# A streaming-encoder block on one core: experts chosen tile by tile inside the mixer, the router fed by transposed h, slot tables built without GpSimd, gates gathered from memory per expert

## The chip, the core and the metric

The kernel runs on one core of one Trainium2 chip. The metric is the device time of one execution in microseconds, as the median of several runs. The core has five engines that work side by side and meet at semaphores: TensorE (PE; PEld is its weight load), VectorE (DVE), ScalarE (ACT), GpSimd (POOL) and SyncE (SP, which here only issues DMAs). PSUM has 8 banks, into which PE writes and from which DVE and ACT read.

## The reference, cut to what matters

One layer over 2048 tokens of width 1024, batch 1, in float32:

```python
u = rms_norm(x, norm1_w)
z = u @ w_in + b_in                      # GLA q,k,v,g, low rank; sliding-window q,k,v
x = x + concat(gla(z), swa(z)) @ w_out   # "the mixer"
hf = rms_norm(x, norm2_w)
gp = softmax(hf @ w_group + b_group)     # 4 groups
g_w, g_idx = top_k(gp, 1)
el = (hf @ w_router + b_router)[group g_idx]   # 8 experts in the chosen group
e_val, e_idx = top_k(el, 2)
gate = softmax(e_val) * g_w
x = x + sum over the 2 chosen of gate * ((silu(hf @ w_gate[e]) * (hf @ w_up[e])) @ w_down[e])
y = rms_norm(x, final_norm_w)
```

There are 32 experts with an inner width of 512; the 2048 tokens make 4096 assignments, 128 per expert on average.

## The kernel before, in words

The program has four stages, each written once per engine.

**The mixer** works on 16 tiles of 128 tokens as a software pipeline: `pipeline` runs turns i = 0, 1, then a loop over pairs for 2 to 15, then 16 and 17. The table `JOBS` gives the PE jobs with their lag (turn i works on tile i - lag), the semaphore that says when a job's PSUM bank has been read, and, by the place in the table, the bank: job k writes bank k mod 8. Before it writes, a job waits (`bank_free`) until the job 8 places earlier (the table taken as a ring that goes on into the turn before) has been read. So a job's place in the table decides whom it waits for. In one turn PE does the projections `qk`, `v`, `g`, `kv`, `qb`, the transposes and small matmuls of both attentions, then `wo0` and `wo1` (output projection), the scores `s0` to `s3`, `bb` and `bl`. DVE adds the output projection to x and gets h (L711), ACT squares h, POOL makes the reciprocal root (L749, L751), DVE scales h to v2 (L738), and SP stores h and v2. In the next turn PE transposes v2 (`u2Ta`, `u2Tb`, L282), DVE copies the transposes to u2T (L638), and PE multiplies them with the router's weights (L373). DVE adds the bias; `logits` keeps all 16 tiles.

**Routing** follows when all 16 tiles are through: DVE picks the group and the two experts for all tiles in one long chain (L922 to L961), PE counts and ranks (L882 to L884), DVE turns ranks into slots and makes two one-hot tables, `place` and `column` (L993), POOL multiplies `column` by token numbers (L1036) and by gates (L1042), and PE sums both over the tokens (L889, L896). The results are, per slot: which token to gather (`idx`), where to add the result (`put`) and its gate (`weight`), and `meta`, the width class of each expert.

**Experts**: a loop over 32 experts. For each, POOL adds back the rows of the expert before (`put_back`, indirect DMA with add, L1087), gathers the rows of the next (L1109 128 rows of 4 KB, L1111 128 quarter rows of 1 KB), and SP loads three weight matrices of 2 MB into one buffer as soon as each has been used. PE does 32 gate matmuls (L1168) and 32 up matmuls (L1179), transposes the next expert's rows (L1136), and does the down projection (L1204). A matmul of float32 shows as two rows, so a group of 32 shows as x64. An expert with up to 128 tokens takes width 128, others 144 or 160; the rest goes to overflow chunks.

**The final norm** reads h back, scales it and stores the output.

Of the kernel before, what the change touches and what calls it, by code (L numbers as in the profile page):

```python
# [17 lines left out]
F32 = mybir.dt.float32  # L18
# [57 lines left out]
class Semaphores:  # L76
# [16 lines left out]
    ("u2Ta", 2, {"u2T_ready": (2, 1)}), ("u2Tb", 2, {"u2T_ready": (2, 2)}),  # L93
# [15 lines left out]
]  # L109
INDEX = {name: k for k, (name, _, _) in enumerate(JOBS)}  # L110


def mixer(nc, sem, bank, A, C, scratch, ctx):
# [23 lines left out]
    xn = sb("xn", [P, D])  # L137
# [10 lines left out]
    la_t = sb("la_t", [P, QKA])  # L148
    g_t = sb("g_t", [P, VA])
    ls = sb("ls_sb", [P, QKA])  # L150
# [26 lines left out]
    def loads(sp):  # L177

        sp.dma_start(x[:, :], A["x"][0:P, :]).then_inc(sem("x_loaded"), 16)
        for lo, hi in ((0, C_V), (C_V, C_G), (C_G, C_LR), (C_LR, IN_W)):  # L180
# [5 lines left out]
            if lo == C_V:  # L186
                sp.wait_ge(sem("xn_ready"), 1)
                sp.dma_start(x[:, :], A["x"][P:2 * P, :]).then_inc(sem("x_loaded"), 16)
# [42 lines left out]
    def sp_iter(sp, i, par):  # L231

        if not isinstance(i, int) or 1 <= i < NT - 1:
            wait_apart(sp, rider, (sem("xn_ready"), i + 1))
            nxt = i + 1 if isinstance(i, int) else (i + 1) & (NT - 1)
            sp.dma_start(x[:, :], tile_rows(A["x"], nxt)).then_inc(sem("x_loaded"), 16)
        if not isinstance(i, int) or i < NT:
            if isinstance(i, int) and i == 1:
                clear_spare(sp)
            wait_apart(sp, rider, (sem("h_stored"), 16 * (i - 1)),  # L240
# [28 lines left out]
    def pe_iter(pe, i, par):  # L269
# [27 lines left out]
        def transpose_x(t):  # L297

            wait(pe, sem("xn_ready"), t + 1)
            transposes("xTa", lambda c: xn[:, c * P:(c + 1) * P], 4)  # L300
            if not (isinstance(t, int) and t == 0):
                on("xTb")
            transposes("xTb", lambda c: xn[:, (4 + c) * P:(5 + c) * P], 4)
# [33 lines left out]
        if on("u2Ta"):  # L337
            wait(pe, sem("v2_ready"), i - 1)
            transposes("u2Ta", lambda c: v2[:, c * P:(c + 1) * P], 4)
        if on("u2Tb"):  # L340
            transposes("u2Tb", lambda c: v2[:, (4 + c) * P:(5 + c) * P], 4)

# [129 lines left out]
        if on("bl"):  # L472
# [3 lines left out]
            m.then_inc(sem("bl_done"), 1)  # L476

# [3 lines left out]
    def act_iter(act, i, par):  # L481
# [51 lines left out]
        if new:  # L533
# [5 lines left out]
            wait(act, sem("ls_ready"), i)  # L539
# [37 lines left out]

    def dve_iter(v_, i, par):
# [5 lines left out]
        def normalise_x(t):  # L584
# [3 lines left out]
            dve.tensor_scalar(xn[:, :], x[:, :], ss[:, 1:2], None, ALU.mult).then_inc(sem("xn_ready"), 1)  # L588
# [101 lines left out]
        if new:  # L690
# [10 lines left out]
            wait(v_, sem("bl_done"), i)  # L701
# [4 lines left out]
        if old:  # L706
            wait(v_, sem("xr_loaded"), 16 * i)
            for n in range(2):
                wait(v_, sem("wo_done"), 2 * (i - 1) + n + 1)
                hs = h[:, 1 - par, n * 512:(n + 1) * 512]  # L710
                dve.tensor_tensor(hs, BK[f"wo{n}"][:, :], hs, ALU.add).then_inc(sem("h_ready"), 1)  # L711
        if new:
# [12 lines left out]
            if isinstance(i, int) and i == 0:  # L725
                dve.memset(sc[:, :, 0:CHUNK], NEG).then_inc(sem("filled"), 1)
                v_.wait_ge(sem("filled"), 6)
# [6 lines left out]
        if old:  # L734
            wait(v_, sem("rstd2_ready"), i)
            wait(v_, sem("v2_stored"), 16 * (i - 1))
            wait(v_, sem("u2Tb_done"), i - 1)
            dve.tensor_scalar(v2[:, :], h[:, 1 - par, :], ss[:, 9:10], None, ALU.mult).then_inc(sem("v2_ready"), 1)  # L738


    def pool_iter(po, i, par):
# [19 lines left out]
        if old:  # L761
# [3 lines left out]
                 (sem("v2_ready"), i - 1))  # L765
# [25 lines left out]
def host_constants():  # L791
# [17 lines left out]
        "c_rank": (j < i).astype(np.float32) - 1.0,  # L809
        "c_tie": np.tile(np.arange(EPG, 0, -1, dtype=np.float32), (P, 1)),  # L810
        "c_cols": np.tile(np.arange(NE, dtype=np.float32) * CAP, (P, 1)),
        "c_ovj": np.arange(NOV, dtype=np.float32)[None, :],
        "c_tok": (1 + np.arange(NT)[None, :] * P + np.arange(P)[:, None]).astype(np.float32),
        "c_rep": np.concatenate([np.tile(np.eye(P, TAIL, dtype=np.float32), (1, P // TAIL)),
                                 np.arange(P, dtype=np.float32)[:, None] // TAIL,
                                 (SEQ + 1 + np.arange(2) * P + np.arange(P)[:, None])], 1).astype(np.float32),
# [4 lines left out]
def routing(nc, sem, bank, A, K, scratch, ctx):  # L821
# [5 lines left out]
    rank_c = sb("rank_c", [P, P])  # L827
    ones = sb("ones", [P, P])
    cols = sb("cols", [P, NE])
    ovj = sb("ovj", [1, NOV])  # L830
    tok = sb("tok", [P, NT])
    iota = sb("iota", [P, P])
    rep = sb("rep", [P, P + 3])
    NCOL = NSLOT // P
    column_t = sb("column_t", [P, 2 * NT, NCOL])
    idx_f = sb("idx_f", [P, NE])
    empty = sb("empty", [P, NCOL])
    put_f = sb("put_f", [P, NCOL])
    spread = sb("spread", [P, 2, NE])
    place = sb("place", [P, 2 * NT, P])  # L840
    column = sb("column", [P, 2 * NT, NCOL])
    lof, hif = sb("slot_lo_f", [P, 2 * NT]), sb("slot_hi_f", [P, 2 * NT])
    gmax, wsum, gw = sb("gmax", [P, NT]), sb("wsum", [P, NT]), sb("gw", [P, NT])
    eg, ohg, pg = sb("eg", [P, NT, NG]), sb("ohg", [P, NT, NG]), sb("pg", [P, NT, NG])
    big = sb("big", [P, NT, NE])
    el, te = sb("el", [P, NT, EPG]), sb("te", [P, NT, EPG])
    oh = sb("oh", [P, 2, NT, EPG])
    mx = sb("mx", [P, 2, NT])
    OH = sb("OH", [P, 2, NT, NE])
    OHs, OHcum = sb("OHs", [P, NE, NT]), sb("OHcum", [P, NE, NT])  # L850
    later = sb("later", [P, NE, NT])
    tot, cnt, nov, cumov, base = (sb(n, [P, NE]) for n in ("tot", "cnt", "nov", "cumov", "base"))
    novi = sb("novi", [P, NE], I32)
    one_row = sb("one_row", [P, NE])
    slot = sb("slot", [P, 2, NT])
    lo, hi = (sb(n, [P, 2, NT], I32) for n in ("slot_lo", "slot_hi"))
    ovc, meta_f = sb("ovc", [1, NOV, NE]), sb("meta_f", [1, NE + NOV + 1])
    logits, gates, dest, idx, meta = K["logits"], K["gates"], K["dest"], K["idx"], K["meta"]
    tie, put, weight = K["tie"], K["put"], K["weight"]

    def sp_loads(sp):

        wait(sp, sem("logits_ready"), NT)
        sp.wait_ge(sem("v2_stored"), 16 * NT)
# [4 lines left out]

    def act_part(act):  # L870
# [666 lines left out]
```

## Time and profile before

| | us |
|---|---|
| median of 3 runs | 1891.57 |
| lowest and highest run | 1891.21 and 1893.16 |
| the profiled execution, its own time | 1888.9 |
| its span, first to last instruction | 1887.0 |
| PE busy in the span | 1768.8 |
| DVE, ACT, POOL busy | 526.2, 495.3, 297.6 |
| mean granted clock of PE | 0.97 |

All durations below come from the profiled execution. Its time is 1.9 us more than its span and 2.7 us less than the median. A busy PE may still work at half its clock, and matmuls overlap each other, so the share of busy time says where PE never waits, not how well it is used. The times of a timeline count from the start of the span.

### The profile page before, as it was taken

How to read it: one execution, taken by the hardware profiler on the slowest of the kernel's cores; microseconds unless marked ns; L12 is line 12 of the kernel's file. 1: busy time of each engine (PE TensorE's matmuls, PEld its weight loads, DVE VectorE, ACT ScalarE, POOL GpSimd, SP SyncE). 2: the span in 40 equal slices, each digit the busy share in tenths (PEclk: the TensorE clock that was granted, in tenths of full speed). 3: DMA queues.
4: the chain of work that ended last, by engine and by line, in shares of the span. 5: the costliest groups of instructions: out<-in, count | busy, mean ns of one | idle time of the engine just before them, and what ended most of it. 6: DMA issues, size and time to landing. Idle time of an engine off the chain costs nothing. (4 is left out here: it accounts for less than half of the span.)

```text
span 1887.0 us, 28465 instructions
## 1 busy us (share of the span) xinstructions
PE 1768.8 (94%) x10628; PEld 1265.9 (67%) x10629; DVE 526.2 (28%) x1089; ACT 495.3 (26%) x1221; POOL 297.6 (16%) x353
## 2 busy tenths in 40 slices
PE   7999999999999999999973899999999999999980
PEld 4556665666656666566642788888888888888860
DVE  1333233332433323342237211111111111111114
ACT  0434343442333433333320111111111111111114
POOL 0000011010110101001012312222222222222223
PEclk9999999999999999999996899999999999999995
DMA  9411011110111001110023489999999899999969
GB/s 325 91 45 46 7 38 44 44 43 2 44 44 44 22 22 44 44 44 11 33 86 108 158 284 330 315 302 313 317 314 328 268 340 314 311 314 316 310 199 361
DMA packets 127760, 312.86 MB, mean 166 GB/s; under 512 B 10179, under 2 KB 18388, under 8 KB 127732
## 3 DMA queue, kind: packets, MB, share of 16 engines
q1 hardware_dynamic: 111460, 269.79, 40.4%
q0 software_dynamic: 15552, 42.61, 9.0%
q8 instruction: 19, 0.31, 0.1%
q10 hardware_dynamic: 720, 0.08, 0.0%
q14 instruction: 9, 0.07, 0.0%
HBM read 265.27 MB, written 47.19 MB: 166 GB/s over the span
## 5 line engine op out<-in xcount | busy, mean ns | idle before, releaser
L287 PE MATMUL bank<-w_in_sb,uT 128*128 128x512 f32 (+1 forms) x1024 | 378.6, 523 | 0.9 <-DVE uT L595 0.9
L287 PEld LDWEIGHTS bank<-w_in_sb,uT 128*128 128x128 f32 x1024 | 176.3, 192 | 168.5 <-issue 168.5
L1168 PEld LDWEIGHTS bank<-xT,wts 128*128 128x128 f32 x2048 | 250.4, 192 | 21.5 <-issue 17.1
L1168 PE MATMUL bank<-xT,wts 128*128 128x128 f32 (+2 forms) x2048 | 254.4, 284 | 3.0 <-issue 1.9
L1179 PE MATMUL bank<-xT,wts 128*128 128x128 f32 (+2 forms) x2048 | 247.9, 282 | 0.0
L1179 PEld LDWEIGHTS bank<-xT,wts 128*128 128x128 f32 x2048 | 245.0, 191 | 0.0
L1204 PE MATMUL bank<-wts,hT 128*128 128x512 f32 x512 | 231.7, 595 | 0.0
L318 PE MATMUL bank<-w_out_sb,mixT 128*128 128x512 f32 x512 | 222.7, 593 | 1.5 <-ACT mixT L517 0.8
L318 PEld LDWEIGHTS bank<-w_out_sb,mixT 128*128 128x128 f32 x512 | 95.9, 190 | 116.5 <-issue 114.3
L1257 DVE TENSOR_TENSOR hT<-bank,sg 128x160 f32<-128x160 f32 x128 | 41.5, 324 | 442.1 <-PE bank L1179 442.1
L1204 PEld LDWEIGHTS bank<-wts,hT 128*128 128x128 f32 x512 | 92.2, 190 | 97.6 <-issue 97.6
L293 PEld LDWEIGHTS bank<-uT,w_in_sb 128*128 128x128 f32 x1280 | 147.9, 192 | 11.9 <-issue 11.6
L293 PE MATMUL bank<-uT,w_in_sb 128*128 128x128 f32 x1280 | 155.7, 277 | 0.0
L749 POOL TENSOR_SCALAR ss<-ss 128x1 f32<-128x1 f32 (+1 forms) x49 | 9.4, 193 | 844.6 <-issue 430.2
L1087 POOL DMA_INDIRECT h_dram<-y,putc x64 | 102.1, 1595 | 35.9 <-POOL putc L1094 26.2
L1223 ACT ACTIVATE y<-bank,gatec 128x256 f32<-128x256 f32 x32 | 15.2, 474 | 344.1 <-PE bank L1204 198.0
L1214 ACT ACT_TABLE_LOAD x32 | 41.1, 1283 | 203.1 <-PE bank L1168 203.1
L1094 POOL COPY putc<-put 128x2 int32 (+1 forms) x32 | 5.9, 184 | 532.9 <-DVE y L1265 532.9
L711 DVE TENSOR_TENSOR h_sb<-bank,h_sb 128x512 f32<-128x512 f32 x32 | 22.1, 692 | 188.3 <-PE bank L318 188.3
L1214 ACT ACTIVATE sg<-bank 128x160 f32<-128x160 f32 x128 | 38.9, 304 | 117.7 <-PE bank L1168 117.3
L574 ACT ACTIVATE sc<-sc,sm 128x192 f32<-128x192 f32 x128 | 56.3, 441 | 32.9 <-DVE sm L733 32.9
L560 ACT ACTIVATE junk<-h_sb 128x1024 bf16<-128x1024 f32 x16 | 16.9, 1057 | 147.8 <-DVE h_sb L711 147.8
(230 smaller groups left out, 1736.5 us busy)
## 6 DMA issues: line engine op xcount, KB each, us to landing
wts<-w_gate_in SPq DMA_DIRECT2D x32, 2048.0 KB, 10.8
wts<-w_up_in SPq DMA_DIRECT2D x32, 2048.0 KB, 9.3
wts<-w_down_in SPq DMA_DIRECT2D x32, 2048.0 KB, 9.0
x_sb<-x_in SPq DMA_DIRECT2D x17, 512.0 KB, 3.7
w_in_sb<-w_in_in SPq DMA_DIRECT2D x4, 2048.0 KB, 12.6
h_sb<-x_in SPq DMA_DIRECT2D x16, 512.0 KB, 4.5
h_dram<-h_sb SPq DMA_DIRECT2D x16, 512.0 KB, 2.7
v_dram<-v_sb SPq DMA_DIRECT2D x16, 512.0 KB, 2.9
```

The source lines that it names most:

```text
L287: m = pe.matmul(bk[name][:, col:col + hi - lo], uT[:, k, :], w_in[:, k, lo:hi], start=k == 0, stop=k == KD - 1)
L293: m = pe.matmul(bk[name][0:hi - lo, col:col + P], w_in[:, k, lo:hi], uT[:, k, :], start=k == 0, stop=k == KD - 1)
L318: m = pe.matmul(bk[f"wo{n}"][:, :], mixT[:, k, :], w_out[:, k, n * 512:(n + 1) * 512], start=k == HA, stop=k == HA - 1)
L560: act.activation(junk[:, :], h[:, 1 - par, :], ACT.Square, accum_out=ss[:, 8:9]).then_inc(sem("ss2_ready"), 1)
L574: act.activation(sc[:, hh, :], sc[:, hh, :], ACT.Exp, bias=nm[:, hh:hh + 1], accum_out=sums[:, hh:hh + 1])
L711: dve.tensor_tensor(hs, BK[f"wo{n}"][:, :], hs, ALU.add).then_inc(sem("h_ready"), 1)
L1087: po.indirect_dma_start(out=table, out_offset=bass.IndirectOffsetOnAxis(ap=putc[:, col:col + 1], axis=0), in_=src, in_offset=None, compute ...
L1168: m = pe.matmul(G[m_ % 2][:, 0:w], wg[:, k, m_ * P:(m_ + 1) * P], xT[:, k, 0:w], start=k == 0, stop=k == KD - 1)
L1179: m = pe.matmul(U[m_ % 2][:, 0:w], wu[:, k, m_ * P:(m_ + 1) * P], xT[:, k, 0:w], start=k == 0, stop=k == KD - 1)
L1204: m = pe.matmul(YB[half][:, :], hT[:, k, 0:P], wd[:, k, half * 512:(half + 1) * 512], start=k == 0, stop=k == KF - 1)
L1214: act.activation(sg[:, m_, 0:n_], G[m_ % 2][:, 0:n_], ACT.Silu).then_inc(sem(pre + "sg_ready"), 1)
L1257: nc.vector.tensor_tensor(hT[:, m_, 0:n_], U[m_ % 2][:, 0:n_], sg[:, m_, 0:n_], ALU.mult)\
```

## The change

It has five parts.

1. PE transposes h itself, not v2. The jobs `u2Ta` and `u2Tb` get lag 1 and move from place 2 and 3 of `JOBS` to its end, after `bl`. The router's output is now multiplied by the reciprocal root when DVE takes it from PSUM, together with the bias.
2. DVE chooses the experts of tile i-2 in turn i, with `choose` in two halves, ahead of the two residual additions. In the last turn both halves run at once, and only then v2 of the last tile is made.
3. x is normalised in place, la_t and ls share one buffer, so the next load of x waits for its transposes; the routing constants are loaded before the last two turns.
4. Routing needs no POOL: token numbers are put into `column` by one instruction per tile and choice (`tensor_scalar` with two operands), only one sum over tokens is left, and the gates are stored to memory by token, 2 for each.
5. In the experts, the gates of a chunk are fetched by two indirect DMAs (`load_gates`, 128 numbers of 4 bytes each) after the put-back of the chunk before.

```diff
 JOBS = [
     ("qk", 0, {"qk_ready": (1, 1)}), ("qdki", 1, {"qdkiT_ready": (1, 1)}),
-    ("u2Ta", 2, {"u2T_ready": (2, 1)}), ("u2Tb", 2, {"u2T_ready": (2, 2)}),
...
     ("bb", 0, {"decays_ready": (1, 1)}), ("bl", 0, {"dec_ready": (1, 1)}),
+    ("u2Ta", 1, {"u2T_ready": (2, 1)}), ("u2Tb", 1, {"u2T_ready": (2, 2)}),
 ]
...
+        for n, name in enumerate(("u2Ta", "u2Tb")):
+            if on(name):
+                wait(pe, sem("h_ready"), 2 * (i - 1) + n + 1)
+                transposes(name, lambda c: h[:, 1 - par, (4 * n + c) * P:(4 * n + c + 1) * P], 4)
...
+        if half == 0:
+            link(dve.tensor_reduce(mt[:, 0:1], L[:, 0:NG], AX.X, ALU.max))
...
+            link(dve.tensor_reduce(tm[:, :], te[:, :], AX.X, ALU.max))
+            return
+        link(dve.tensor_scalar(oh[:, 0, :], te[:, :], tm[:, :], None, ALU.is_equal))
...
+        dve.tensor_tensor(at(OHcum, t + 1), at(OHcum, t), at(OHs, t), ALU.add).then_inc(sem("choose_steps"), 1)
...
-            dve.tensor_tensor(dst, BK["router"][:, 0:NR], b_r[:, :], ALU.add).then_inc(sem("logits_ready"), 1)
+            wait(v_, sem("rstd2_ready"), i - 1)
+            dve.scalar_tensor_tensor(logits[:, :], BK["router"][:, 0:NR], ss[:, 9:10], b_r[:, :], ALU.mult, ALU.add)\
+                .then_inc(sem("logits_ready"), 1)
...
             for n in range(2):
+                if old2:
+                    if n == 0:
+                        wait(v_, sem("logits_ready"), i - 1)
+                    choose(v_, i - 2, n)
                 wait(v_, sem("wo_done"), 2 * (i - 1) + n + 1)
...
         for g in range(0, 2 * NT, PART):
-            for onehot, n, number in ((place, P, lof), (column, NCOL, hif)):
...
+            dve.tensor_tensor(place[:, g:g + PART, :], iota[:, None, :].to_broadcast([P, PART, P]),
+                              lof[:, g:g + PART].unsqueeze(2).to_broadcast([P, PART, P]), ALU.is_equal)
+            for n in range(g, g + PART):
+                m = dve.tensor_scalar(column[:, n, :], iota[:, 0:NCOL], hif[:, n:n + 1], tok[:, n:n + 1], ALU.is_equal, ALU.mult)
+            m.then_inc(sem("columns_ready"), 1)
...
+    def sp_gates(sp):
+        sp.wait_ge(sem("gates_ready"), 1)
+        sp.dma_start(scratch["gate"].rearrange("(t p n) o -> p t (n o)", p=P, n=2), gates[:, :, :]).then_inc(sem("gates_stored"), 16)
...
+    def load_gates(po, pre, at):
+
+        for part in range(2):
+            po.indirect_dma_start(out=gatec[:, part:part + 1], in_=scratch["gate"], out_offset=None,
+                                  in_offset=bass.IndirectOffsetOnAxis(ap=slotc[:, at + part:at + part + 1], axis=0))\
+                .then_inc(sem(pre + "gate_loaded"), 16)
...
+        put_back(po, "m_", y[:, 0, :], 0)
+        put_back(po, "m_", yt, 1, quarters=True)
+        load_gates(po, "m_", 2)
```

How PE's program stands in the loop over tiles, from the transposes of qd and ki to the `v` projection, before (L282 are `u2Ta` and `u2Tb`, L348 the GLA scores `att`, L359 the state update `dS`, L287 the `v` projection):

```order
L282 MATMUL bank<-ident,v_sb 128x128 [waits v2_ready,s_taken]
L282 MATMUL bank<-ident,v_sb 128x128 x3
L60 REGISTER_ALU
L282 MATMUL bank<-ident,v_sb 128x128 [waits s_taken]
L282 MATMUL bank<-ident,v_sb 128x128 x3
L60 REGISTER_ALU
L60 REGISTER_ALU [waits s_taken]
L348 MATMUL bank<-qdkiT 128x128 [waits qdkiT_ready,s_taken]
L348 MATMUL bank<-qdkiT 128x128 x3
L359 MATMUL bank<-v_sb,ke 64x128 [waits dec_ready,ke_ready,decays_ready,first_consts]
L359 MATMUL bank<-v_sb,ke 64x128 x7
L287 MATMUL bank<-w_in_sb,uT 128x512 [waits qdkiT_ready]
```

The same place now (line numbers of the changed kernel: L332 and L334 for qd and ki, L341 `att`, L352 `dS`, L286 the `v` projection):

```order
L332 MATMUL bank<-ident,qd 128x128 [waits qdki_ready,s_taken]
L332 MATMUL bank<-ident,qd 128x128
L334 MATMUL bank<-ident,ki 128x128 x2
L60 REGISTER_ALU
L60 REGISTER_ALU [waits s_taken]
L341 MATMUL bank<-qdkiT 128x128 [waits qdkiT_ready,s_taken]
L341 MATMUL bank<-qdkiT 128x128 x3
L352 MATMUL bank<-v_sb,ke 64x128 [waits dec_ready,ke_ready,decays_ready,first_consts]
L352 MATMUL bank<-v_sb,ke 64x128 x7
L60 ISA
L286 MATMUL bank<-w_in_sb,uT 128x512 [waits u2T_ready]
L286 MATMUL bank<-w_in_sb,uT 128x512 x7
```

The eight transposes are gone from between ki and `att` (they stand behind `bl`, ahead of the `qk` projection), and the `v` projection, which waited for the copy of qdkiT, now waits for u2T: it uses the bank of `u2Tb`. DVE's program has the two copies to u2T where they were, after the products with the softmax's sums and the addition to qk.

POOL's program in the loop over experts, before (copy of the gather's numbers, two gathers, copy of the put-back's numbers, two put-backs):

```order
L1122 COPY idxc<-idx 128x2
L66 REGISTER_ALU
L1109 DMA xg<-v_dram,idxc 128x1024 [waits m_index_ready,meta_ready]
L1111 DMA xg<-v_dram,idxc 128x256
L66 REGISTER_ALU
L1070 REGISTER_ALU [waits meta_ready,m_y_put]
L1070 REGISTER_ALU [waits m_yA_taken]
L1094 ISA [waits m_yD_taken]
L1094 COPY putc<-put 128x2
L1087 DMA h_dram<-y,putc 2304x1024 [waits m_put_index_ready,meta_ready]
L1087 DMA h_dram<-y,putc 9216x256
```

And now:

```order
L1118 COPY idxc<-idx 128x2
L66 REGISTER_ALU
L1105 DMA xg<-v_dram,idxc 128x1024 [waits m_index_ready,idx_ready]
L1107 DMA xg<-v_dram,idxc 128x256
L66 REGISTER_ALU
L1046 REGISTER_ALU [waits idx_ready,m_y_put]
L1046 REGISTER_ALU [waits m_yA_taken]
L1069 ISA [waits m_yD_taken]
L1069 COPY slotc<-tables 128x4
L1063 DMA h_dram<-y,slotc 2304x1024 [waits m_rows_ready,idx_ready]
L1063 DMA h_dram<-y,slotc 9216x256
L1075 DMA gatec<-gate_dram,slotc 128x1 x2
```

Two gathers of single numbers stand behind the put-backs, and so ahead of the gathers of the next turn.

## Rows read from the trace of the kernel before

**Rows 1.** Windows: stretch, length, busy us by engine (PE, PEld, DVE, ACT, POOL), clock, DMA share, GB/s.
```profile
200.00:300.00 100.00, 100.00 (x544) 64.13 (x543) 33.32 (x67) 37.51 (x92) 9.75 (x14) 1.00 0.07 27
...
980.00:1020.00 40.00, 14.57 (x43) 8.67 (x41) 22.23 (x58) 1.62 (x4) 0.74 (x2) 0.66 0.42 150
```

**Rows 2.** Timeline of one tile: start, us, engine, line, out<-in, idle before it.
```profile
898.92 0.38 PE L335 MATMUL bank<-ident,ki 128*128 128x128 f32 x2
...
899.14 1.04 PE L282 MATMUL bank<-ident,v_sb 128*128 128x128 f32 x8
...
899.34 0.60 ACT L495 ACTIVATE qdkiT<-bank 128x512 f32<-128x512 f32 x1
...
900.11 0.72 PE L348 MATMUL bank<-qdkiT 64*128 64x128 f32 x8
...
901.35 7.13 PE L287 MATMUL bank<-w_in_sb,uT 128*128 128x512 f32 x16
...
902.35 1.27 DVE L638 TENSOR_TENSOR u2T<-bank,norm_sb 128x512 f32<-128x512 f32 x2
```

**Rows 3.** Timeline: first tile's attention, and the second expert's start.
```profile
65.45 1.23 PE L348 MATMUL bank<-qdkiT 64*128 64x128 f32 x8 [2.94 <-ACT qdkiT L495]
...
67.67 8.78 PE L287 MATMUL bank<-w_in_sb,uT 128*128 128x512 f32 x16
...
1080.03 9.03 PE L1168 MATMUL bank<-xT,wts 128*128 128x128 f32 x64 [1.92 <-issue]
```

**Rows 4.** Timeline: DVE's residual additions in the loop and in the last tile.
```profile
882.24 0.69 DVE L711 TENSOR_TENSOR h_sb<-bank,h_sb 128x512 f32<-128x512 f32 x1 [5.58 <-PE bank L318]
...
985.22 0.69 DVE L711 TENSOR_TENSOR h_sb<-bank,h_sb 128x512 f32<-128x512 f32 x1 [2.67 <-PE bank L318]
```

**Rows 5.** Timeline from the last router matmuls to the first expert.
```profile
991.62 3.60 PE L373 MATMUL bank<-w_r_sb,u2T 128*128 128x36 f32 x16 [0.87 <-DVE u2T L638]
...
1008.97 2.08 PE L882 MATMUL bank<-OHs,rank_c 128*128 128x512 f32 x2 [13.76 <-DVE tot L961]
...
1013.28 0.18 DVE L966 TENSOR_SCALAR novi<-cnt 128x32 int32<-128x32 f32 x1
...
1014.85 0.69 DVE L976 TENSOR_SCALAR big<-bank 128x512 f32<-128x512 f32 x1
...
1021.27 1.22 DVE L993 TENSOR_TENSOR place<-iota,slot_lo_f 128x1024 f32<-128x1024 f32 x1
...
1023.43 1.22 DVE L993 TENSOR_TENSOR place<-iota,slot_lo_f 128x1024 f32<-128x1024 f32 x1
...
1052.16 1.04 PE L1136 MATMUL bank<-ident,xg 128*128 128x128 f32 x8
```

**Rows 6.** Timeline of one 128-wide expert: gathers, and transposes of what they bring.
```profile
1183.30 1.03 POOL L1109 DMA_INDIRECT xg<-v_dram,idxc  x1 [0.85 <-POOL idxc L1122]
...
1184.63 0.99 POOL L1111 DMA_INDIRECT xg<-v_dram,idxc  x1 [0.30 <-issue]
...
1191.18 1.04 PE L1136 MATMUL bank<-ident,xg 128*128 128x128 f32 x8
```

**Rows 7.** Windows: that expert, and one of width 144.
```profile
1176.60:1199.10 22.50, 22.50 (x155) 18.45 (x154) 3.82 (x9) 3.64 (x8) 5.58 (x6) 1.00 1.02 337
...
1226.50:1252.30 25.80, 25.80 (x187) 20.79 (x186) 3.82 (x9) 3.75 (x8) 5.59 (x6) 1.00 0.88 295
```

**Rows 8.** DMA view, 1183.25 to 1183.6 us: tile, queue, count, us from issue to landing.
```profile
xg<-v_dram,idxc POOLq DMA_INDIRECT x1, 7.4
```

**Rows 9.** DMA view, 1180.6 to 1181 us: the second put-back of that turn.
```profile
h_dram<-y,putc POOLq DMA_INDIRECT x1, 8.0
```

**Rows 10.** DMA view, 960 to 1100 us: the gathers ahead of and in the first experts.
```profile
xg<-v_dram,idxc POOLq DMA_INDIRECT x6, 4.5
```

**Rows 11.** DMA view, 30 to 60 us: packets by size; the queue's share of 16 engines.
```profile
DMA packets 5129, 7.14 MB, mean 238 GB/s; under 512 B 2769, under 2 KB 3153, under 8 KB 5128
...
q1 hardware_dynamic: 5128, 7.13, 95.0%
```

More of the change, by code:

```diff
@@ L854, in routing @@
[L854 to L859, printed above, removed]
+    groups, gates, idx, meta = K["groups"], K["gates"], K["idx"], K["meta"]
+    OH, OHs, OHcum, tops = K["OH"], K["OHs"], K["OHcum"], K["tops"]
@@ L861, in sp_loads @@
+    tables = K["tables"][:, :].rearrange("p (c f) -> p c f", f=4)
+    pairs = lambda t: t.rearrange("p (n b) -> p n b", b=2)
+    flat = lambda t: t.rearrange("p a b -> p (a b)")
     def sp_loads(sp):
-        wait(sp, sem("logits_ready"), NT)
-        sp.wait_ge(sem("v2_stored"), 16 * NT)
         for dst, src in ((rank_c[:, :], A["c_rank"]), (cols[:, :], A["c_cols"]),
@@ new lines, in dve_part @@
+        v_.wait_ge(sem("slot_sums"), 1)
+        found = bank[2][:, 0:NCOL]
+        link(dve.tensor_scalar(tables[:, :, 0:2], pairs(found), -1.0, 0.0, ALU.add, ALU.max))
+        link(dve.tensor_single_scalar(pairs(idx), tables[:, :, 0:2], 1, ALU.logical_shift_right))
+        dve.tensor_copy(spread[:, 0, :], idx[:, 1:2 * NE:2])
+        dve.tensor_copy(spread[:, 1, :], tables[:, 0:NE, 1]).then_inc(sem("spread_args"), 1)
+        link(dve.tensor_copy(tok_f[:, :], idx))
+        v_.wait_ge(sem("slot_sums"), 2)
@@ new lines, in dve_part @@
+        dve.tensor_scalar(idx[:, 1:2 * NE:2], bank[3][:, 0:NE], 4.0, rep[:, P:P + 1], ALU.mult, ALU.add)\
+            .then_inc(sem("idx_ready"), 1)
+        dve.tensor_copy(tables[:, 0:NE, 1], bank[3][:, NE:2 * NE]).then_inc(sem("puts_ready"), 1)
+        v_.wait_ge(sem("route_exps"), 1)
+        link(dve.tensor_reduce(wsum[:, :], pg[:, :, :], AX.X, ALU.add))
+        link(dve.scalar_tensor_tensor(wsum[:, :], e2[:, :], 1.0, wsum[:, :], ALU.add, ALU.mult))
+        link(dve.reciprocal(gates[:, :, 0], wsum[:, :]))
@@ new lines, in dve_part @@
+        dve.tensor_tensor(gates[:, :, 1], gates[:, :, 0], e2[:, :], ALU.mult).then_inc(sem("gates_ready"), 1)
+        link(dve.scalar_tensor_tensor(pairs(empty[:, :]), pairs(found), 0.0,
+                                      rep[:, None, P + 1:P + 3].to_broadcast([P, NCOL // 2, 2]), ALU.is_equal, ALU.mult))
+        link(dve.tensor_tensor(put_f[:, :], tok_f[:, :], empty[:, :], ALU.add))
+        dve.tensor_copy(spread[:, 2, :], put_f[:, 1:2 * NE:2]).then_inc(sem("spread_args"), 1)
+        dve.tensor_copy(tables[:, :, 2:4], pairs(put_f[:, :])).then_inc(sem("puts_ready"), 1)
@@ L1261, in dve_y @@
         if part or pre == "m_":
-            after(v_, pre, "gate_ready", n + 1)
+            wait(v_, sem(pre + "gate_loaded"), 32 * (n + 1))
             after(v_, pre, "y_free", n)
```

384 lines of the change are left out of this document (169 added, 215 removed).

## The prediction

> **What bounds the kernel now.** I read the windows by stage first. From 200 to 300 us PE is busy for all of 100 us at full clock, while the DMA engines stand at 7% [rows 1]: the mixer is bound by PE, and any wait put into PE's program there is paid in full, once per tile. From 980 to 1020 us PE works for 14.57 of 40 us and its clock is 0.66 [rows 1]: that is routing, bound by a chain over DVE, PE and POOL. In the experts PE is again busy throughout, 22.50 of 22.50 us for an expert of width 128, but there the DMA engines are full as well, 1.02 of their time; at width 144 an expert takes 25.80 us and DMA 0.88 of it [rows 7]. So three stages answer to the change in three ways, and I cost each by itself, against the profiled execution's 1888.9 us.
>
> **Mixer: what the moved transposes uncover.** The second half of the transposes of ki begins at 898.92 and takes 0.38, the eight transposes of v2 follow at 899.14, and `att` starts at 900.11 [rows 2]. They last about as long as ACT's copy of qdkiT, which starts at 899.34, takes 0.60 and is what `att` waits for [rows 2]. Now they stand ahead of the `qk` projection, so everything from there on is 0.97 us later (899.14 to 900.11), and ki's end is at 899.30 + 0.97 = 900.27. The copy then runs from 900.3 to 900.9, and `att` starts at 901.05 after the 0.17 that lie between the copy's end and `att` today. PE does the same work and loses 0.94.
>
> The second wait is larger. The `v` projection starts at 901.35 today [rows 2], with `att` 0.94 later it could start at 902.3. But it now uses the bank of `u2Tb` and waits for the second copy to u2T. DVE makes these copies from 902.35 to 902.35 + 1.27 = 903.62 [rows 2], after work that hangs on the softmax's exponentials and not on PE's transposes, and nothing in the change brings that work forward. With 0.15 for the semaphore, `v` starts at 903.77 instead of 901.35: 2.42 us per tile, the 0.94 within it. It happens in each turn that has both a `v` and an older u2T, i = 2 to 15: 14 x 2.42 = **+33.9 us**. Behind `v` nothing gives it back, since PE has no idle time in a turn.
>
> In turn 1 PE waits 2.94 us for that copy and then runs cold, `att` taking 1.23 and `v` 8.78 us where a warm turn has 0.72 and 7.13 [rows 2, 3]. There the transposes of tile 0 now fill 0.97 of the wait, which may keep the clock: 0 to -2.2, I take **-1**.
>
> **Mixer: what is hidden.** `choose` gives DVE 9 and 11 small instructions per tile. Linked instructions on 32 elements follow each other every 0.22 us (7 from 1013.28 to 1014.85 [rows 5]), so the halves take 2.0 and 2.4 us. DVE sits idle for 5.58 us ahead of the first residual addition, and ahead of the second for 2.67 even in the last tile [rows 4]. Cost nothing; were the cover gone, it would be 4.4 x 15. Loading x later costs nothing either: SP issues it after the store of v2 in any case. In the last turn the `v` wait does not exist.
>
> **Routing.** From the last residual addition, which ends at 985.22 + 0.69 = 985.91 [rows 4]: today the chain goes over ACT, POOL, v2 and the transposes, and the router's matmuls start at 991.62, cold, 3.60 us long [rows 5]. Now four transposes (0.5) and a copy of 0.7 follow, and the router starts near 987.6. I take 2.4 us for it, between a warm half of 3.60 and 3.60: 990.0. Logits and both halves of `choose` for the last tile, 0.2 + 18 links x 0.22 + 0.4 = 4.6: 994.6. PE counts (0.5), then ranks, 2.08 for one pair of passes [rows 5] and nearly as much for the other, 3.6 in all; DVE's chain of 7 links over the counts (1.6) lies beside them: 998.7. Slot arithmetic: two instructions over 1024 elements at 1.25, three over 512 at 0.7, five links at 0.22 = 5.7, where today it takes 6.4 (1014.85 to 1021.27 [rows 5]): 1004.4. The one-hot tables: a first pair (2 x 1024 elements, POOL idle) goes from 1021.27 to 1023.43 [rows 5], 2.16, four pairs 8.6; with 28 more instructions at about 0.06, 10.4, ending at 1014.8. Nobody multiplies on POOL, so PE sums 1.0 behind the last group, five links and a matmul give `idx` 1.7 later, and POOL issues the first gather at 1018.6. It lands in 4.5 [rows 10], plus 0.7 because the store of the gates (2048 pieces of 8 bytes) runs beside it: first transposes at 1023.8 instead of 1052.16 [rows 5]. **-28 us**, from -22 (tables at twice the price) to -33. Loads of the first expert's weights are issued once v2 is stored and have 20 us, so they hide.
>
> **Experts: two more DMAs in a full queue.** POOL issues a gather every 1.33 us (1183.30, 1184.63), and the gather for the next expert, 7.4 us in flight [rows 8], lands at 1190.7 for transposes that start at 1191.18 [rows 6]. That is a margin of 0.48; over the 15 experts of width 128 with this pattern it is 0.45 on average, of which some 0.3 can be used up. The gate loads go ahead of the gather in program order and in the same queue. Below: the engine time of 256 packets. At width 128 the engines moved 337 GB/s x 22.5 us = 7.6 MB in 1.02 x 16 x 22.5 = 367 us of engine time [rows 7], 0.048 us per KB. From 30 to 60 us 5128 packets took 95% of 16 x 30 = 456 us [rows 11]; with 329 us for their 6.8 MB in large pieces, the 2769 packets under 512 B are left with 46 ns each. So 256 take 256 x 0.046 / 16 = 0.7 us: 15 x (0.7 - 0.3) = 6. Above: the issue slips by 2 x 1.33 = 2.66 and the packets come on top, 3.4: 15 x 3.1 + 9 x 1.5 (width 144, where half of the 3.3 us that such an expert takes more [rows 7] stand ahead of the transposes, a margin of 1.9) + 2 = 62. Between: the queue works in order. The second put-back, issued at 1180.67, lands 8.0 later [rows 9], at 1188.7, the gather of 8 packets per engine 2.0 behind it, or, with the 8 of the quarter rows that follow and are through 0.5 later, about 0.15 us per packet of an engine, which shares its time with the weights' packets. The 16 gate packets per engine at that rate are 2.2 to 2.5 us. This is the nearest row, and I take 2.2: 15 x 1.9 + 9 x 0.3 + 1 = **+32 us**.
>
> The Trainium skill (DMA: Bandwidth & Descriptors, section Bandwidth) gives a floor of about 10.5 ns per packet for a small transfer. By it 256 packets would take 2.7 us per expert and the term would be some +45. The trace's 46 ns over 16 engines, 3 ns per packet, doesn't agree with it, and the sum goes by the trace.
>
> **Sum**: +33.9 - 1 - 28 + 32 = +37 us: 1926 for the profiled execution, and on the scale of the median, 1891.57, **1928 us**.
>
> **Rivals.**
> (All times on the median's scale.) *A, the forecast*: both waits as costed, 48%. Its own range, with -33 to -22 for routing and +11 to +55 for the experts, is 1903 to 1957.
> *B, the clock falls in every tile*, 20%. `att` stands between two waits of 0.8 and 1.4 us. For it: turn 1, where 2.94 us of waiting left PE at half its clock [rows 3]. Against: after 1.92 us of idling the second expert's matmuls run warm (9.03 for 64 of width 160) [rows 3]. Price: (1.23 - 0.72) for `att`, as much for `dS`, and 8.78 - 7.13 for `v`, 2.6 x 14 = 37: 1965. The Trainium skill (TensorE: Matmul & The Clock Gate, section on HAM oscillation) describes a kernel that waits once in each turn and starts each turn cold. By that rule the time would be the 1965 just given.
> *C, the gathers stay nearly hidden*, 15%: the gate packets slip into gaps of the put-backs. For it: the put-backs are in flight for 8.0 us, so a later issue need not mean a later landing. Against: the DMA engines are full at width 128. Experts 0 to +6: 1896 to 1903.
> *D, the other side: the `v` projection does not wait*, 9%. It takes one thing, that DVE has copied u2T by 902.3, which needs ACT's exponentials 1.4 us sooner than in the trace. Then the mixer costs 14 x 0.94 = 13, and with the gathers at their lower bound the sum is 13 - 1 - 28 + 6 = -10: 1882. It decides from there on, and with the experts at +16 or more even this ends no faster.
> The remaining 8% are causes not listed, on either side.
>
> **How the numbers follow.** The prediction is A's time. The range reaches from C's lower end to past B, 1898 to 1974: it leaves out D, the last part of B and the rest, 2 in 10. A change under 0.2%, 4 us, can't be told from none. Faster: half of D and a part of the rest, 0.08. Same: the other half of D and a bit of C, 0.06. Slower: 0.86.
>
> **What would show it.** In the tile loop PE should idle about 0.8 us ahead of `att`, released by ACT's copy, and about 1.4 ahead of `v`, released by DVE's copy to u2T; the distance between tiles should go from 59.6 to 62.0 us. If `v` starts without idling, D is right; if `v` takes over 8 us in each turn, B. The first transposes of gathered rows should come 28 us sooner after the last residual addition. In experts of width 128 the distance should be 24.4 and not 22.50 us, with PE idle ahead of the transposes; if it stays 22.50, C. The prediction would be wrong altogether if the copies to u2T came before the exponentials, or if the gather's landing did not move.

## The result: slower by 4.8%, and the profile after

The changed kernel takes 1982.16 us (median of 4 runs, 1978.98 to 1988.53) against 1891.65 us before, beside it on the same chip (1891.21 to 1893.16): a ratio of 1.0484, 95% interval 1.046 to 1.0507. Slower was right; the size was not: the forecast was 1928, and the time lies 8 us above the top of the range.

I cut both profiled spans at the same four events: the start of the last residual addition (1025.89 us after, 985.22 before [rows 4]), the first transposes of gathered rows (1072.43, and 1052.16 before [rows 5]), the start of the last expert's evacuation of y (1923.9, 1833.4 before) and the end.

| part of the span, us | before | after | difference | forecast |
|---|---|---|---|---|
| mixer | 985.2 | 1025.9 | +40.7 | +33.9 - 1 |
| routing, up to the first transposes | 66.9 | 46.5 | -20.4 | -28 |
| experts | 781.3 | 851.5 | +70.2 | +32 |
| last expert's put-back and final norm | 53.6 | 55.4 | +1.8 | 0 |
| span | 1887.0 | 1979.3 | +92.3 | +37 |

The windows that answer to [rows 1] (columns as there):

```profile
200.00:300.00 100.00, 97.77 (x532) 62.29 (x532) 35.49 (x99) 35.43 (x89) 7.18 (x12) 1.00 0.06 21
980.00:1020.00 40.00, 31.64 (x163) 20.85 (x162) 17.78 (x45) 12.28 (x39) 4.49 (x6) 0.79 0.25 88
```

PE, which was busy for all of 100 us in the mixer, now idles for 2.23 of them. The chain of waits of the changed kernel's PE names the places (what waited, for what: us in sum, times, longest):

```profile
PE bank L1132 <- DMA xg<-v_dram,idxc: 48.0, 25, 4.3
PE bank L286 <- DVE u2T L679: 19.8, 14, 1.5
PE bank L341 <- ACT qdkiT L492: 14.1, 16, 1.8
```

Before, the first of these rows does not exist, and in the tile loop neither do the others (outside it `att` waits 2.94 us, once [rows 3]). L1132 are the transposes of gathered rows, L286 the `v` projection, L341 `att`.

**Mixer.** Timeline of PE and of the two copies ahead of it, in the turn that answers to [rows 2]:

```profile
933.91 0.38 PE L334 MATMUL bank<-ident,ki 128*128 128x128 f32 x2
...
934.33 0.60 ACT L492 ACTIVATE qdkiT<-bank 128x512 f32<-128x512 f32 x1 [0.78 <-PE bank L334]
...
935.07 0.71 PE L341 MATMUL bank<-qdkiT 64*128 64x128 f32 x8 [0.78 <-ACT qdkiT L492]
...
936.50 1.28 DVE L679 TENSOR_TENSOR u2T<-bank,norm_sb 128x512 f32<-128x512 f32 x2
937.84 7.13 PE L286 MATMUL bank<-w_in_sb,uT 128*128 128x512 f32 x16 [1.45 <-DVE u2T L679]
```

Both waits are there near the forecast size: 0.78 and 1.45 in this turn, 0.86 and 1.37 in every other one, 2.23 in sum. Between most tiles the distance went from 59.6 to 61.9 us. But 4 of the 14 distances are 63.6, and there the same projection is longer (second line: the window of that projection, columns as in [rows 1]):

```profile
188.29 8.83 PE L286 MATMUL bank<-w_in_sb,uT 128*128 128x512 f32 x16 [1.46 <-DVE u2T L679]
188.29:197.12 8.83, 8.83 (x19) 3.89 (x19) 1.73 (x6) 0.00 (x0) 0.00 (x0) 0.81 0.00 0
```

8.83 us for the matmuls that take 7.13 elsewhere: the granted clock was 0.81 in them, so part of them ran at 1.2 GHz, the lower of PE's two clock levels, and not at 2.4.

**Experts.** POOL's timeline ahead of one 128-wide expert, and PE's in that expert and the next, which answer to [rows 6]:

```profile
1160.35 1.02 POOL L1075 DMA_INDIRECT gatec<-gate_dram,slotc  x1 [0.30 <-issue]
1161.68 0.98 POOL L1075 DMA_INDIRECT gatec<-gate_dram,slotc  x1 [0.30 <-issue]
...
1163.65 0.97 POOL L1105 DMA_INDIRECT xg<-v_dram,idxc  x1 [0.80 <-POOL idxc L1118]
```
```profile
1170.92 1.09 PE L1132 MATMUL bank<-ident,xg 128*128 128x128 f32 x8 [1.81 <-DMA xg<-v_dram,idxc]
1171.84 3.60 PE L1200 MATMUL bank<-wts,hT 128*128 128x512 f32 x8
...
1196.65 1.97 PE L1132 MATMUL bank<-ident,xg 128*128 128x128 f32 x8 [3.02 <-DMA xg<-v_dram,idxc]
1198.41 5.62 PE L1200 MATMUL bank<-wts,hT 128*128 128x512 f32 x8
```

The reader is to see three things. PE stands until the rows of the gather of 1163.65 are there, 7.3 us after its issue, about as long in flight as before [rows 8]. The wait of 1.81 us leaves the matmuls warm (1.09, 3.60). The one of 3.02 us is paid again: the transposes take 1.97 and the first down matmuls 5.62 us, 2.9 us more: the granted clock was 0.50 in the transposes and 0.64 in the down matmuls. Of the 25 waits in the table, those up to 2.62 us were followed by transposes of 1.09; of the six from 2.90 up, four were followed by 1.96 or 1.97, one (3.90) by 1.72 and one (3.15) by 1.20.

**Routing.** The timeline that answers to [rows 5], from the store of the gates to the first expert:

```profile
1061.19 0.37 SPq L916 DMA_DIRECT2D gate_dram<-gates  x1
...
1061.71 1.22 POOL L1105 DMA_INDIRECT xg<-v_dram,idxc  x1 [0.94 <-POOL idxc L1118]
...
1072.43 1.94 PE L1132 MATMUL bank<-ident,xg 128*128 128x128 f32 x8 [10.04 <-issue]
```

The first gather is issued 35.8 us behind the last residual addition (60.2 before, 33.4 forecast), but from there to the first transposes 10.7 us go by, for which the forecast had 5.2.

### The profile page after: what moved, and what is told of

It reads as the page before. It is cut to its first block and busy times, and to the rows that moved or that the text cites. A ratio compares the mean times of both kernels' runs of the same rounds, so it can differ in the third digit from the quotient of the medians.

```text
span 1979.3 us, 28970 instructions
## 1 busy us (share of the span) xinstructions
PE 1786.2 (90%) x10564; PEld 1266.9 (64%) x10565; DVE 568.0 (29%) x1408; ACT 492.9 (25%) x1189; POOL 344.2 (17%) x412
## 5 line engine op out<-in xcount | busy, mean ns | idle before, releaser
L286 PE MATMUL bank<-w_in_sb,uT 128*128 128x512 f32 (+1 forms) x1024 | 383.8, 529 | 23.1 <-DVE u2T L679 19.8
L286 PEld LDWEIGHTS bank<-w_in_sb,uT 128*128 128x128 f32 x1024 | 178.5, 194 | 195.8 <-issue 170.1
L1200 PE MATMUL bank<-wts,hT 128*128 128x512 f32 x512 | 239.2, 611 | 0.0
L1063 POOL DMA_INDIRECT h_dram<-y,slotc x64 | 103.0, 1610 | 35.9 <-POOL slotc L1069 26.2
L1132 PE MATMUL bank<-ident,xg 128*128 128x128 f32 x330 | 53.5, 298 | 58.2 <-DMA xg<-v_dram,idxc 48.0
L1069 POOL COPY slotc<-tables 128x4 int32 (+2 forms) x33 | 6.1, 185 | 520.5 <-DVE y L1258 520.5
L1132 PEld LDWEIGHTS bank<-ident,xg 128*128 128x128 f32 x330 | 42.1, 153 | 80.5 <-issue 80.5
L1075 POOL DMA_INDIRECT gatec<-gate_dram,slotc x66 | 65.9, 999 | 20.6 <-issue 19.8
```

The costliest lines, as they stand in the source:

```text
L286: m = pe.matmul(bk[name][:, col:col + hi - lo], uT[:, k, :], w_in[:, k, lo:hi], start=k == 0, stop=k == KD - 1)
L1063: po.indirect_dma_start(out=table, out_offset=bass.IndirectOffsetOnAxis(ap=slotc[:, at:at + 1], axis=0), in_=src, in_offset=None, compute_ ...
L1075: po.indirect_dma_start(out=gatec[:, part:part + 1], in_=scratch["gate"], out_offset=None, in_offset=bass.IndirectOffsetOnAxis(ap=slotc[:, ...
L1132: m = pe.transpose(XB[j % 2][:, c * P:(c + 1) * P], src, ident)
L1200: m = pe.matmul(YB[half][:, :], hT[:, k, 0:P], wd[:, k, half * 512:(half + 1) * 512], start=k == 0, stop=k == KF - 1)
```

## The experiments

The theories after this reading: (1) the experts' loss is the order of issue on POOL, two gate loads ahead of the two gathers; the rival is the gate loads' 256 packets, wherever they are issued. (2) The mixer's loss is the new place of `u2Ta` and `u2Tb`, of which the larger part is DVE's copy; rivals are a clock that falls for the `att` wait alone, and `choose` on DVE. (3) Routing's shortfall is the store of the gates, which shares the DMA engines with the first gathers. ("y" stands below for the start of DVE's evacuation of y, and the gather's time behind it is the median over the experts.) Eight kernels ran, four on one chip, where the kernel before took 1889.14 us (gate loads behind, shorter delay, copies earlier, old place), and four on another, where it took 1888.08. Except for the last, each has one run, and is compared with the changed kernel by its profiled span; the five that leave the mixer as it is in the changed kernel show it within 1.9 us of each other, on both chips.

### Gate loads behind the gathers

```diff
         put_back(po, "m_", yt, 1, quarters=True)
-        load_gates(po, "m_", 2)
...
                 gather(po)
+                load_gates(po, "m_", 2)
                 scattered(po, "m_", e)
```

> The changed kernel, but POOL issues the two gate loads of an expert behind the two gathers of rows for the next one, no longer ahead of them. Theory 1 (the gathers come late because two issues of 1.16 us stand ahead of them on POOL): the first gather is again issued about 6.5 us after y is taken (9.06 in the changed kernel), TensorE's waits for the gathered rows shrink from 48 us to near those of the kernel before, the expert part shrinks from 851 us to between 785 and 800, and the time is 1915 to 1932 us. Rival (the 256 small packets of the gate loads hold the gathers up in the DMA queues): the loads still run beside the gathers, the expert part stays above 835 us and the time above 1965.

Measured: 1919.78 us, span 1917.9, 61.4 less than the changed kernel. Experts 791.4 us (851.5), the gather 6.5 us behind y (9.06). The wait that was 48.0 us:

```profile
PE bank L1131 <- DMA xg<-v_dram,idxc: 1.0, 3, 0.4
```

Theory 1 holds. The same loads at another place in POOL's program cost 10.1 us over the kernel before, and not 70. (The recorded 1.16 us per issue is too low: the gather was issued 2.6 us later for two of them, 1.3 each.) POOL's timeline of one expert shows them behind:

```profile
1162.30 1.01 POOL L1104 DMA_INDIRECT xg<-v_dram,idxc  x1 [0.85 <-POOL idxc L1117]
1163.62 0.99 POOL L1106 DMA_INDIRECT xg<-v_dram,idxc  x1 [0.30 <-issue]
1164.91 0.96 POOL L1075 DMA_INDIRECT gatec<-gate_dram,slotc  x1 [0.31 <-issue]
1166.18 0.95 POOL L1075 DMA_INDIRECT gatec<-gate_dram,slotc  x1 [0.30 <-issue]
```

The rival's 256 packets are not in the traces. The DMA view of one 128-wide expert, from its first gate matmul to the next expert's, in the kernel before (1176.64 to 1199.14 us) and in the changed one (1154.41 to 1178.93):

```profile
DMA packets 3074, 7.57 MB, mean 337 GB/s; under 512 B 112, under 2 KB 240, under 8 KB 3074
```
```profile
DMA packets 3153, 7.62 MB, mean 311 GB/s; under 512 B 176, under 2 KB 304, under 8 KB 3152
```

With the gate loads 64 packets under 512 B more pass in an expert, where the forecast and the rival had reckoned 256.

### A delay on POOL in their place

```diff
         put_back(po, "m_", yt, 1, quarters=True)
+        for half in range(2):
+            nc.gpsimd.tensor_tensor(idle[:, half, :, :], four, four, ALU.mult)
```

> As the kernel with the gate loads behind the gathers, but where they stood ahead of them POOL multiplies two 128x464 tiles that nobody reads (1.15 us each as an estimate from 1.27 us for 128x512): the delay of the gathers without any packets ahead of them. Theory 1 (POOL's issue order): the gathers are again about 9 us behind y, the expert part 845 to 855 us, 1975 to 1990 us. Rival (packets of the gate loads): as the kernel with the gate loads behind, whatever that gives, at most 10 us above it.

Measured: 1935.89 us, span 1934.1, experts 810.3. My estimate for the multiplications was too high, they moved what follows by 0.91 us each: the gather slipped to 8.3 us behind y, by 1.83 and not 2.6, so neither number was met, and the run says only that 1.83 us of slip without a packet cost 19 us over the kernel with the gate loads behind. Theory 1 had said 1975 or more, but for a slip that the kernel did not have. Hence one with the right length.

### The delay at full length

```diff
-    idle = sb("idle", [P, 2, 4, 116])
-    four = ident[:, None, 0:116].to_broadcast([P, 4, 116])
+    idle = sb("idle", [P, 2, 6, 110])
+    four = ident[:, None, 0:110].to_broadcast([P, 6, 110])
```

> As the kernel with the delay on POOL (gate loads behind the gathers, two multiplications that nobody reads ahead of them), but these are 128x660 in place of 128x464, so that the gathers slip by the 2.58 us by which they slip in the changed kernel; at 464 they slipped by 1.83 us, and the expert part took 810 us. Theory (the slip alone decides, and beyond waits of some 1.5 us TensorE's clock falls too, which makes the last 0.75 us of slip dear): waits for gathered rows of 40 to 50 us in sum, the expert part 840 to 855 us, 1970 to 1985 us. Rival (the slip costs only itself, and the rest of the changed kernel's loss comes from the gate loads' packets ahead of the gathers): the expert part 820 to 832 us, 1945 to 1958 us.

Measured: 1971.11 us, span 1969.2, experts 843.2, gather 8.95 us behind y. PE's chain of waits, of this kernel and (second row) of the one with the shorter delay:

```profile
PE bank L1135 <- DMA xg<-v_dram,idxc: 44.6, 26, 2.4
```
```profile
PE bank L1135 <- DMA xg<-v_dram,idxc: 17.1, 16, 1.5
```

| slip of the gather behind y, us | experts, us | waits for rows, us |
|---|---|---|
| 0 (before) | 781.3 | 0 |
| 0.04, gate loads behind | 791.4 | 1.0 |
| 1.83, delay on POOL | 810.3 | 17.1 |
| 2.49, longer delay | 843.2 | 44.6 |
| 2.6, the changed kernel | 851.5 | 48.0 |

The slip alone makes 51.8 of the 60.1 us between the second and the last row. The remaining 8.3 go with the loads' place ahead of the gathers (and 0.1 us of slip). One run stands for the longer delay, and in the five kernels with the loads ahead the experts took 848.8 to 854.0 us, so these 8.3 may be 5.6 to 10.8. In the changed kernel there are waits of 2.9 to 4.3 us and the slow matmuls behind them; here the longest was 2.4, and one wait (1.92) was followed by slow transposes (1.66 us). The other traces agree: each of the five kernels with the loads ahead has two to six waits of 2.9 us or more, none of the four with the loads behind has one of more than 2.4. One of these waits (3.90 here) follows a gather that POOL issues 1 us later than the others, in the same expert in all five; what holds the others up is open. So the theory's first half holds and its second does not: it had put the steep last 0.66 us down to the clock. The expert distances show what it is. Of the fifteen experts that take 22.50 us before, the last has no successor to wait for; the others go to 23.4 to 24.2 with the shorter delay and to 24.5 to 26.8 with the longer. The nine that take 25.8 have room for a slip of 1.83 (seven stay at 25.8 to 26.0), and with 2.49 take 27.3 to 29.5. Of the 33 us between the two delays 15 are in these nine and 16 in the fourteen. The same shows in the start of the transposes behind y: in 128-wide experts 16.3 us with the longer delay, 7.3 behind the gather's issue, but in the first four 144-wide ones 17.0 to 17.8, so that there the rows take 8.1 to 8.8 us from the gather's issue, and with the shorter delay it was back within 7.3. What the later gather meets in the wider experts was not tested.

### The u2T copies earlier on DVE

```diff
+            if old2:
+                copy_u2()          # the two copies bank -> u2T
             wait(v_, sem("exps_ready"), i)
...
-        if old2:
-            for n, name in enumerate(("u2Ta", "u2Tb")): ...   # their old place
```

> The changed kernel, but VectorE takes the two u2T copies out of the banks ahead of its wait for ScalarE's exponentials (2.1 us idle in every tile), no longer behind it. Theory 1 (the v projection waits 1.45 us for the u2T copy, and this wait on top of the 0.78 us before att is what lets the clock fall in 4 of 14 turns): tile distance 60.4 to 60.6 in all 14 turns, no turn of 63.6, mixer 25 to 28 us shorter, about 1955 us. Rival 1 (the clock falls for the att wait alone): some turns stay 1.7 us longer, 1960 to 1966. Rival 2 (what VectorE does later is late by what the copies take, and the v projection waits for something else): distance near 61.9, 1978 to 1985.

Measured: 1953.38 us, span 1951.5, distances 60.36 to 60.46 in all 14 turns, mixer 995.6 (1025.9), 30.3 us shorter where 25 to 28 were expected (2.0 of them in the last turn). The timeline of a turn, the `v` projection now without a wait:

```profile
908.25 0.72 PE L341 MATMUL bank<-qdkiT 64*128 64x128 f32 x8 [0.78 <-ACT qdkiT L492]
908.90 0.67 PE L352 MATMUL bank<-v_sb,ke 64*64 64x128 f32 x16
909.50 7.13 PE L286 MATMUL bank<-w_in_sb,uT 128*128 128x512 f32 x16
```

Theory 1 holds: 1.45 us per turn (1.37 in every other one) was DVE's copy, and without it no turn falls to the lower clock although the `att` wait is still there.

### The transposes of h at their old place

```diff
     ("qk", 0, ...), ("qdki", 1, {"qdkiT_ready": (1, 1)}),
+    ("u2Ta", 2, {"u2T_ready": (2, 1)}), ("u2Tb", 2, {"u2T_ready": (2, 2)}),
...
-    ("u2Ta", 1, {"u2T_ready": (2, 1)}), ("u2Tb", 1, {"u2T_ready": (2, 2)}),
 ]
```

(with `wait(pe, sem("h_ready"), 2 * (i - 2) + n + 1)` and `h[:, par, ...]`, between ki and `att` as before.)

> The changed kernel, but the transposes u2Ta and u2Tb stand at their old place between qdki and att (still of h, with the weights applied in the copy and the factor in the logits). Theory 1 (all that the mixer lost per turn comes from this place: 8 transposes of about 0.8 us that covered ScalarE's qdkiT copy, and the copy u2T ahead of v): tile distance 59.6 as in the kernel before, the mixer 33 to 41 us shorter, 1941 to 1950 us. Rival (the choice of experts and the longer chain on VectorE cost part of it): distance 60.2 or more, 1955 or more.

Measured: 1939.23 us, span 1937.4, distances 59.56 to 59.63, the very ones of the kernel before; mixer 985.65 us against 985.22. (The time lies 2 us under the expected 1941 to 1950, the mixer's 40.2 us within its 33 to 41.) Its timeline has the old cover again:

```profile
897.99 1.04 PE L281 MATMUL bank<-ident,h_sb 128*128 128x128 f32 x8
898.96 0.71 PE L345 MATMUL bank<-qdkiT 64*128 64x128 f32 x8
```

All that a turn of the mixer lost is this place; `choose`, the logits' factor and the shared buffers cost nothing there.

### The first half of the choice three times

```diff
-CHOOSE_STEPS = 18
+CHOOSE_STEPS = 36
...
-        if half == 0:
+        if half < 3:
...
-                choose(v_, i - 2, n)
+                choose(v_, i - 2, 2 * n)          # parts 0, 1, 2: the first half
+                choose(v_, i - 2, 2 * n + 1)      # part 3: the second
```

> The changed kernel, but the first half of the choice of experts is done three times over in each tile (18 operations and 4.2 us more on VectorE; the results are the same). Theory (VectorE does the choice in idle time that it has ahead of the two residual additions, 3.7 us and 3.5 us): tile distances as in the changed kernel, 61.9 and at times 63.6; only the last tile's choice, behind its router, is on the path: 4.2 us more in all, 1983 to 1989 us. Rival (the choice adds to the length of a tile): distances above 62.5, 1995 us or more.

Measured: 1987.97 us, span 1985.7, +6.4. Distances 61.9 and three of 63.6 as before, mixer 1025.7 us; routing 51.5 in place of 46.5. The theory holds; of the 4.2 us expected behind the last router, 5.0 came, and the rest of the 6.4 is experts (+1.7), which the edit does not touch and which differ by up to 5.2 us between kernels with the same expert stage. DVE still idles 1.65 us ahead of the first residual addition (3.68 in the changed kernel), with 4.2 us more work in the turn:

```profile
914.99 0.69 DVE L761 TENSOR_TENSOR h_sb<-bank,h_sb 128x512 f32<-128x512 f32 x1 [1.65 <-PE bank L317]
```

### The gates stored after the first gathers

```diff
         sp.wait_ge(sem("gates_ready"), 1)
+        sp.wait_ge(sem("m_xg_loaded"), 16)
+        sp.wait_ge(sem("m_xt_loaded"), 16)
```

> The changed kernel, but SP stores the gates (2048 pieces of 8 bytes), and loads the final norm's weights behind them, only after the first expert's two gathers have landed. Theory (the store's pieces share the DMA engines with the first gathers, so that these take 10.7 us from issue to the first transpose and not some 5): first transposes 39 to 43 us behind the last residual addition in place of 46.5, time 3 to 6 us shorter, 1974 to 1979 us. Rival (the first gathers take that long by themselves, after the change of the order of the tables): no change there, and 0 to 5 us more where the gate loads wait for the later store.

Measured: 1977.19 us, span 1975.3, routing 40.7 us in place of 46.5:

```profile
1060.97 1.22 POOL L1107 DMA_INDIRECT xg<-v_dram,idxc  x1 [0.94 <-POOL idxc L1120]
...
1065.72 1.94 PE L1134 MATMUL bank<-ident,xg 128*128 128x128 f32 x8 [3.84 <-issue]
```

From issue to transposes 4.75 us, not 10.7. The edit holds back two transfers, the store and the 512 KB of the final norm's weights, issued at 1065.32 in the changed kernel. Its DMA views tell them apart (the lines give packets, MB and the share of the 16 engines' time). From 1062 to 1064 us the 2064 packets of the store pass, and no others, in 46.6% of the engines' time, 7 ns each. From 1064 to 1069 packets of the gathers pass, and no others (first line; second line: this kernel's from 1062 to 1066):

```profile
q0 software_dynamic: 68, 0.28, 72.4%
```
```profile
q0 software_dynamic: 191, 0.66, 53.5%
```

With the store ahead a packet of the gathers takes 0.724 x 16 x 5 / 68 = 0.85 us of an engine; without it 0.18. The theory holds as to the cause: it is the store, since no packet of the weights is among these 68. The store's packets themselves do not keep the engines from the gathers': they are through before the first of the gathers starts, and it is the gathers' own packets that are slow until the store has landed, 8.6 us after its issue; from 1069 to 1073 they take 0.21 us again. Why is not shown.

### The three together

The first, fifth and seventh edit in one kernel; what stays is the choice in the mixer, the router on transposes of h, the shorter routing and the gates from memory.

> The changed kernel with three edits at once: the gate loads behind the gathers, u2Ta and u2Tb at their old place, and the gates stored after the first gathers. What stays of the change is the choice in the mixer, the router's transposes of h, the shorter routing and the gates from memory. By the sum of the single edits (-62 and -43 us measured, -3 to -6 for the store): 1871 to 1880 us, faster than the kernel before by 0.6 to 1%. Rival (with the edits together TensorE's stronger clock or the earlier gathers collide with the weights): 1885 us or more.

Measured, 5 runs: 1873.07 us (1871.67 to 1877.30) against 1888.08 (1886.28 to 1890.74, 9 runs); ratio 0.9923, 95% interval 0.991 to 0.9937: 0.8% under the kernel before, a small gain, but clear of noise, and as expected. Its profiled span is 12.3 us shorter: mixer +1.1, routing -26.3, experts +12.9, the end 0. Tile distances are 59.6 again, and waits for gathered rows 3.2 us in sum.

## Why the prediction was wrong in size

**Mixer, 14 x 2.42 us: right.** Measured 2.23 us of waits and 2.3 of distance, 32 us in 14 turns; the two steps (ACT's copy uncovered, DVE's copy late because it hangs on the exponentials) are shown apart by the fourth and fifth experiment. Rival D is out: `v` did wait.

**Rival B, the clock falls in every tile: right in kind, not in extent.** It fell in 4 of 14 turns and cost 1.7 us in each (8.83 - 7.13), 6.8 us against the 37 of the rival. The forecast's sum had nothing for it: the text gave the chance to all turns or none and missed the case between. The Trainium skill (TensorE: Matmul & The Clock Gate, section on HAM oscillation) describes the kernel that starts every turn cold; here 4 turns of 14 did, with waits of the same sum in each, so the trace agrees in kind and not in regularity. Which turns fall is open: between runs of the same mixer they are different ones.

**The first and last turns: off by little.** The 14 turns in the loop make 2.3 x 14 + 6.8 = 39, the last turn 4.2 (40.81 for 36.62), which the text had put at nothing ("In the last turn the `v` wait does not exist"). There `att` waits 1.82 us where it had no wait before; it is slow, 1.23 us, in both kernels. With the transposes at their old place the last turn took 38.2, and 39.65 in the last experiment, so 1.6 to 3.0 of the 4.2 are not the place; what they are is open. Turns 0 and 1 gave back 2.5, where 1 was forecast: `att` and `v` of turn 1 ran warm (0.71 and 7.13).

**`choose` hidden: right**, shown by the old place and by tripling its first half.

**Routing, -28 forecast, -20.4 measured.** The step that failed is "plus 0.7 because the store of the gates (2048 pieces of 8 bytes) runs beside it": the store cost 5.9 us (46.5 to 40.7). With it moved, routing gives -26.3, for the most part the forecast less the tables, whose 8 groups took 12.8 us (1.60 each) where 10.4 were reckoned. The error was to price the 2048 pieces by the engines' time for them. That time is 7 ns each, even less than the 46 ns which the text had got as a remainder; what the pieces cost is the time of the gathers' packets behind them, 0.85 us for 0.18.

**Experts, +32 forecast, +70 measured: the step that made the prediction wrong.** The step that failed is the one that begins "Between: the queue works in order". It took 2.2 us per expert for the gate packets ("15 x 1.9 + 9 x 0.3 + 1"), and left the 2 x 1.33 us of later issue to the upper bound. It was the other way round. The 16 gate packets per engine that it priced are 4 in the view (64 for 16 engines), and the issue slip of 2.6 us is paid in full: a gather is in flight for 7.3 us (median over the experts) when it starts early, 7.3 with the longer delay and 7.7 in the changed kernel. By the delay experiment the slip makes 52 of the 70 us. "A later issue need not mean a later landing", rival C's support, is refuted by the same run.

Term by term the 70 us are these. The fifteen experts of 22.50 us gained 45.9 (28.5 forecast). Eight of them came out at 24.4 to 24.6, the distance that the text had named, and that was luck: it had taken 2.2 us of packets less a margin of 0.3, and what came was 2.6 us of slip less the margin of 0.5. One took 25.3, the last has no successor to wait for, and five took 27.3 to 29.3, each with a wait of 2.9 us or more ahead of the next rows, and in four of them slow transposes (1.72 to 1.96 us) behind it. The nine of width 144 gained 13.9 (2.7 forecast): their margin of 1.9 is there (with a slip of 1.83 seven of them keep their distance), but beyond it the loss was 1.0 to 2.5 us each. The remaining 10.4 (1 forecast) are the expert with the wait of 3.02, 5.9 (28.6 for 22.7), the first two of the five widest, 3.5, and 1.0 elsewhere. The upper bound of 62 came near the first two terms (46.5 and 13.5; the first by luck, since it set 0.7 us of packets on top of the slip in each expert, and what came on top were the long waits in five) and missed the third, 2 for 10.4.

10 us stay in the experts even with the gathers on time, where the forecast had a lower bound of 6: 2.9 in the first two of the five widest experts (27.4 us to 28.9 and 28.8), 3.5 spread over the fifteen of 22.50, 1.8 in two of the nine, 2.0 ahead of the first expert's y. What makes them is not shown.

**The end, 0 forecast, +1.8.** It is there in all five kernels with the gate loads between the put-backs and the gathers (55.4 to 56.1 us) and not in the four with the loads behind the gathers (53.4 to 53.8, before 53.6).

## What to carry to other kernels

When DMAs are added to a program that issues them from an engine, cost first the later issue of the next one in that program that somebody waits for, in full, and only then the packets; issuing the new ones behind it made 61 us of difference here. A block of work that covers another engine's copy is not free to move: look for what starts in its shadow on both sides, the consumer behind it and the bank's new owner. And a store of many tiny pieces just ahead of the first transfer of a new stage can cost that stage its start, however little engine time its packets take: here holding it back until the transfer had landed gave 5.9 us.

## What the runs showed that I had not expected

- PE waits of up to 2.4 us, one in an expert, leave its clock at the upper level in 25 of 26 cases with the longer delay; the two waits of 0.78 and 1.45 us with 1.3 us of small matmuls between them cost it the level in 4, 4, 4, 3, 3 and 3 of 14 turns in six runs, and never when only the `att` wait was left. No length of wait divides the cases: waits of 1.93 and 2.01 us were followed by slow transposes (1.62 and 1.32) in two other runs, one of 3.16 by fast ones (1.09) in a third.
- 2048 pieces of 8 bytes (16 KB), issued 0.5 us ahead of a gather of 128 rows of 4 KB, made that gather 5.9 us later. Their own packets took 7 ns each and were gone by then; the gather's took 0.85 us in place of 0.18.
- Two loads of 128 numbers of 4 bytes add 64 packets to an expert in the DMA view, not 256.
- The price of a late gather is not linear: 19 us for 1.8 us of slip, 52 for 2.45, over the kernel with the gate loads behind.
- Two multiplications of 128x464 on POOL moved what follows by 0.91 us each, where those of 128x512 with two different sources take 1.27.
